# Down matrices of 29 experts requested from ScalarE's queue instead of SyncE's

## The reference

```
x = x + merged @ w_out
h2 = rmsnorm(x)
# 32 experts, the best 4 for each token, softmax weights over the 4
gu  = h2[tokens of e] @ w_gu[e] + b_gu[e]           # 1024 -> 2048
hid = (clip(lin) + 1) * g * sigmoid(1.702 * g)      # g, lin: halves of gu, clamped at 7
y   = hid @ w_down[e] + b_down[e]                   # 1024 -> 1024
x   = x + sum over the 4 experts of weight * y
out = rmsnorm(x)
```

## Time and profile before

| | |
|---|---|
| median of 3 executions | 1201.55 us (1201.41 to 1204.66) |
| the profiled execution | 1201.84 us, its span 1200.0 us |
| TensorE busy | 1113.0 us, 93% |
| VectorE, ScalarE busy | 401.2 and 246.9 us |
| SyncE's queue | 449.79 of the 452.07 MB moved |
| transfers of expert matrices | 83 up (52 of 4096 KB, 17 of 2048, 14 of 1024) and 72 down (56 of 2048 KB, 16 of 1024) |
| mean granted clock of TensorE | 0.98 of full speed |

### The profile page before, as it was taken

One profiled execution on the slowest core, in us unless ns is written; L12 is line 12 of the kernel. 1 busy time (PEld: TensorE's weight loads), 2 busy tenths in 40 slices (PEclk: granted clock), 3 DMA queues, 4 the chain that ended last, 5 costly groups with the idle time before them and its releaser, 6 DMA issues.

```text
span 1200.0 us, 14789 instructions
## 1 busy us (share of the span) xinstructions
PE 1113.0 (93%) x6062; PEld 590.1 (49%) x6062; DVE 401.2 (33%) x695; ACT 246.9 (21%) x389; POOL 4.5 (0%) x10
## 2 busy tenths in 40 slices
PE   8999999999999989898989989889899998998995
PEld 8999999985444333333333333333344333333331
DVE  6767554563322222222222222222222222222212
ACT  6344674433111111111111111111111111111112
POOL 0000000000000000000000000000000000000000
PEclk9999999999999999999999999999999999999998
DMA  9984343689999999999999999999999999999994
GB/s 332 349 280 142 116 160 132 251 313 372 415 421 430 431 430 430 431 431 430 431 432 429 430 436 433 426 435 431 427 435 429 429 434 423 432 435 424 427 404 193
DMA packets 60119, 452.07 MB, mean 377 GB/s; under 512 B 3458, under 2 KB 34423, under 8 KB 40247
## 3 DMA queue, kind: packets, MB, share of 16 engines
q1 hardware_dynamic: 59408, 449.79, 91.0%
q0 software_dynamic: 560, 1.74, 0.5%
q10 hardware_dynamic: 119, 0.08, 0.0%
HBM read 450.53 MB, written 1.06 MB: 376 GB/s over the span
## 4 chain that ended last, share of the span: by engine, by line
PE 48%; DMA 48%; SPq 1%; issue 1%; DVE 1%; ACT 1%; DVEq 0%; ACTq 0%
DMA dring<-in_w_down_dram 41%; PE bank L1111 17%; PE bank L1433 13%; PE bank L1394 11%; DMA ring<-in_w_gu_dram 6%; PE bank L1361 2%; DMA ring<-in_w_mem_kv_dram 1%; PE bank L1312 1%; PE bank L1336 0%; PE bank L1340 0%; PE bank L1201 0%; PE bank L1181 0%; PE bank L1409 0%; PE bank L1212 0%; ACT w_high L469 0%
## 5 line engine op out<-in xcount | busy, mean ns | idle before, releaser
L1394 PE MATMUL bank<-ring,region_x 128*64 128x512 f32 x2048 | 456.3, 597 | 8.0 <-DMA ring<-in_w_gu_dram 8.0
L1433 PE MATMUL bank<-dring,region_r 128*64 128x512 f32 x1024 | 245.6, 631 | 60.2 <-DMA dring<-in_w_down_dram 59.9
L1394 PEld LDWEIGHTS bank<-ring,region_x 128*64 128x64 f32 x2048 | 141.2, 137 | 282.6 <-issue 266.1
L1433 PEld LDWEIGHTS bank<-dring,region_r 128*64 128x64 f32 x1024 | 74.2, 144 | 229.6 <-issue 135.3
L1111 PE MATMUL bank<-hT_high,w_high 128*128 128x256 f32 x384 | 110.1, 287 | 1.4 <-DVE hT_low L708 1.4
L1111 PE MATMUL bank<-hT_low,w_high 128*128 128x256 f32 x384 | 108.6, 283 | 0.0
L1111 PE MATMUL bank<-hT_high,w_low 128*128 128x256 f32 x384 | 108.6, 283 | 0.0
L1050 DVE SCALAR_TENSOR_TENSOR y_parts<-bank,region_r,y_parts 64x512 fp32r<-64x512 f32 x32 | 23.8, 744 | 249.5 <-ACT y_parts L642 249.5
L716 DVE TENSOR_TENSOR w_low<-ring,w_high 128x2048 fp32r<-128x2048 f32 x39 | 89.3, 2289 | 53.3 <-ACT w_high L469 53.1
L1031 DVE TENSOR_SCALAR region_r<-bank 128x512 f32<-128x512 f32 x32 | 22.1, 692 | 252.3 <-PE bank L1394 252.3
L469 ACT ACTIVATE w_high<-ring 128x2048 fp32r<-128x2048 f32 x39 | 74.5, 1912 | 62.5 <-PE bank L1111 57.8
(11 more groups left out here) (237 smaller groups left out, 887.9 us busy)
## 6 DMA issues: line engine op xcount, KB each, us to landing
ring<-in_w_gu_dram SPq DMA_DIRECT2D x52, 4096.0 KB, 26.3
dring<-in_w_down_dram SPq DMA_DIRECT2D x56, 2048.0 KB, 24.7
ring<-in_w_gu_dram SPq DMA_DIRECT2D x17, 2048.0 KB, 11.5
ring<-in_w_in_dram SPq DMA_DIRECT2D x26, 1024.0 KB, 11.9
dring<-in_w_down_dram SPq DMA_DIRECT2D x16, 1024.0 KB, 12.3
ring<-in_w_gu_dram SPq DMA_DIRECT2D x14, 1024.0 KB, 8.2
ring<-in_w_out_dram SPq DMA_DIRECT2D x4, 1024.0 KB, 5.0
ring<-in_w_mem_kv_dram SPq DMA_DIRECT2D x3, 1024.0 KB, 11.9
```

Of the source, the lines that this page charges most:

```text
L1394: last = mm(ps[64 * half:64 * half + 64, :], xg[u // 2][:, c, 64 * (u % 2):64 * (u % 2) + 64], ring[:, slot0 + c, k * F + half * 512:k * F ...
L1433: last = mm(y_ps[64 * half:64 * half + 64, :], lhsT, dring[:, c // 2, at:at + 512], start=(c == 0), stop=(c == KC - 1))
```

## The change

SyncE no longer asks for the down matrices of experts 1 to 29; it asks for the up matrices alone, and for the downs of experts 0, 30 and 31 as before. The interleaved order of experts 22 to 29 is gone with them. ScalarE asks for the down matrix of expert s+1 in `weighted_high(s)`, when it has waited for the whole down product s, between its two weighting instructions, as two transfers of two slots each. Its loop ends two rounds earlier, and the last rounds are written out without requests. In TensorE's stream only the counts change that `down` waits for, as down matrix 1 no longer comes in single slots.

```diff
@@ -388,31 +388,14 @@
             for c, n in ((0, 1), (1, 1), (2, 1), (3, 1), (4, 1), (5, 1), (6, 2)):
                 sp.wait_ge(pieces_used, N_MIX + (expert - 2) * KC + c + n)
                 up_chunks(expert, slot0 + c, c, n)
-        expert_down(1, 1, 1)
-
         with sp.Fori(0, more * (E // 2) + (E // 2 - 7)) as i:
             expert_up((i * 2 + 4) % E, 8, i * 16 + (N_MIX - RING + 33))
-            expert_down((i * 2 + 2) % E, i * 8 + 5)
             expert_up((i * 2 + 5) % E, 0, i * 16 + (N_MIX - RING + 41))
-            expert_down((i * 2 + 3) % E, i * 8 + 9)
 
         ups, downs = more * (KC * E) + (N_MIX - RING + 1), more * (DRING * E) + (1 - DRING)
-
-        def half_up(expert, h):
-            sp.wait_ge(pieces_used, ups + expert * KC + 4 * h + 3)
-            up_chunks(expert, 8 * (1 - expert % 2) + 4 * h, 4 * h, 4)
-
-        for expert in range(E - 10, E - 5):
-            half_up(expert, 0)
-            expert_down(expert - 2, downs + (expert - 2) * DRING)
-            half_up(expert, 1)
-        expert_down(E - 7, downs + (E - 7) * DRING)
-        for expert in range(E - 5, E - 2):
-            half_up(expert, 0)
-            half_up(expert, 1)
-            expert_down(expert - 1, downs + (expert - 1) * DRING)
+        for expert in range(E - 10, E - 2):
+            expert_up(expert, 8 * (1 - expert % 2), ups + expert * KC)
         expert_up(E - 2, 8, ups + (E - 2) * KC, 2)
-        expert_down(E - 3, downs + (E - 3) * DRING)
         for c, n in ((0, 2), (2, 2), (4, 2), (6, 1), (7, 1)):
             sp.wait_ge(pieces_used, ups + (E - 1) * KC + c + n - 1)
             up_chunks(E - 1, c, c, n)
@@ -634,21 +617,30 @@
             act.wait_ge(y_ready, s + 1)
             act.activation(unused, y_ps[:, 0:TT * P], ACT.Copy, accum_out=w_slot).then_inc(w_slot_ready, 1)
 
-        def weighted_high(s):
+        def weighted_high(s, following):
 
             act.wait_ge(downs_used, (s + 1) * DRING)
             act.wait_ge(w_slot_ready, s + 1)
             act.activation(y_parts[0:64, 0:512], y_ps[0:64, :], ACT.Copy, scale=w_slot[0:64, :])
+            if following is not None:
+                for m in range(2):
+                    act.dma_start(dring[:, 2 * m:2 * m + 2, :].rearrange("p k n -> p (k n)"),
+                                  a["w_down"][0, bass.ds(following, 1), m * 512:(m + 1) * 512, :]
+                                  .rearrange("e (p k) n -> p (e k n)", k=4)).then_inc(down_in[2 * m], 16)
             act.activation(y_parts[64:128, 512:1024], y_ps[64:128, :], ACT.Copy, scale=w_slot[64:128, :])\
                 .then_inc(y_high, 1)
 
         sigmoid_of(0)
-        with act.Fori(0, more * E + (E - 1)) as s:
+        with act.Fori(0, more * E + (E - 3)) as s:
             hidden_and_slots(s)
             sigmoid_of(s + 1)
-            weighted_high(s)
+            weighted_high(s, (s + 1) % E)
+        for s in range(E - 3, E - 1):
+            hidden_and_slots(more * E + s)
+            sigmoid_of(more * E + (s + 1))
+            weighted_high(more * E + s, None)
         hidden_and_slots(more * E + (E - 1))
-        weighted_high(more * E + (E - 1))
+        weighted_high(more * E + (E - 1), None)
 
 
         act.activation(norm[:, 3, 4:6], norm[:, 1, 2:4], ACT.Sqrt)
@@ -1468,7 +1460,7 @@
                 s = i * 4 + u
                 nxt = (i, u + 1) if u < 3 else (i + 1, 0)
                 up(*nxt, False, lambda: small_products(i, u))
-                down(s, int(u > 0))
+                down(s, 0)
                 begin(s + 2)
                 next_half(*nxt)
 
@@ -1482,13 +1474,13 @@
                     for half in range(2):
                         mm(acc[t][half][:, :], wexpT[:, t * P:(t + 1) * P], b_down[:, half * 512:half * 512 + 512],
                            start=False, stop=False)
-            down(s, 1 + u // 2)
+            down(s, u // 2)
             if u < 2:
                 begin(s + 2)
             if u < 1:
                 next_half(i, u + 1)
         small_products(i, 3, 1)
-        down(i * 4 + 3, 3)
+        down(i * 4 + 3, 2)
 
         pe.wait_ge(y_ready, more * E + (E + 1))
         pe.wait_ge(scaT_sb, more * E + (E + 1))
```

## The result

The changed kernel takes 1236.1 us (median of 4, 1233.7 to 1239.2) against 1202.7 for the kernel before: a ratio of 1.0281, 95% interval 1.0257 to 1.0305, slower by 33 us. Forecast was slower, by 19, with a range up to 1225; the loss is 1.8 times the forecast.

The account below looks back on a forecast made before the run. The 16 DMA engines were taken to bound the expert stage; 19 us later at down product 30, 1.5 of them from the start, gave a span of 1200 + 19, or 1220.5 us on the median's scale, range 1205 to 1225.

Parts of the forecast that it names:

- What bounds the kernel, and R: DMA engines bound the expert stage; R is up-matrix data outstanding, in us of DMA time, when a down product ends.
- R(28): Up-matrix data outstanding at the end of down product 28: 35.4 us before, forecast 12.9 (10 to 14).
- the sum for the start: At the start, down matrix 1 is asked for later: DMA idle for 0 to 2.6 us, 1.5 taken.
- Lead in the tail: Tail: down product 30 starts at 1185.8 instead of 1166.75, 19 us later, 1.5 of them from the start.
- the prediction's first rival: Requests are served in order of asking, two queues or one: down product 30 at 1186.9, time 1221.7; chance 0.12.
- Turns by packet: Queues alternate by packet: down matrices get one third of the rate beside up halves; 1216 to 1224, chance 0.55.
- Turns by whole transfers: Queues alternate up half, down half: loss 11.9 us, time 1213.5; chance 0.10.
- equal bytes: Queues share by bytes: downs always in time, TensorE waits for up second halves; +4.8, time 1206.4; chance 0.10.
- a higher rate: Two queues hide gaps between packets: 436 against 431 GB/s, 9.4 us; 1197 with the lead kept, chance 0.08.
- Issue on ScalarE: Two requests per expert between the weighting halves: y_parts 0.7 to 1.4 us later, 5.1 us of cover, cost 0.
- The steady state: Main loop: outstanding up data fall from 15.6 to about 6 us, swing between some 2 and 8; DMA stays busy.
- the prediction's rule: Main loop: down gets a third until outstanding ups are gone, all the rate until 11.7 us, then a third again.

Follow-up runs that it names:

- e11: The changed kernel run once more unaltered, for a second profile: 1233.3 us.
- e1: The kernel before, one queue, with SyncE keeping the plain order of its loop from expert 22 on: 1219.0 us, ratio 1.0134.
- e4: The changed kernel, but SyncE asks for the down matrices from expert 20 on in the interleaved order of the kernel before: 1217.1 us, ratio 1.0113.
- e2: The changed kernel with up matrices from expert 4 on in pieces of 2 slots, 16 KB packets like the downs: 1210.6 us, ratio 1.0067.
- e3: The changed kernel with ScalarE's down matrices in single slots, 8 KB packets beside 32 KB up packets: 1269.6 us, ratio 1.0579.
- e5: The changed kernel, but ScalarE asks for the first half of the next down matrix in the middle of the down product: 1220.7 us, ratio 1.0162.
- e7: The kernel before, one queue, with up matrices from expert 4 on in pieces of 2 slots: 1205.8 us, ratio 1.0038.
- e8: The kernel before, one queue, with both down halves asked for only after the whole down product: 1201.5 us, ratio 1.0001.
- e9: The kernel before with b_down asked for early on ScalarE's queue and the 8 bias products moved ahead of down product 29: 1201.1 us, ratio 0.9988.

## Why the prediction was right in kind and too small

**What bounds the kernel, and R.** Right. Down product 30 started 1201.9 - 1156.8 = 45.1 us after the end of down product 28, forecast 45.7, without a wait. R(28) = 1177.2 - 9.7 - 1156.8 = 10.7, forecast 12.9 (10 to 14); that is by landing, as in the prediction. One small slip in the sum for the start: 1024 KB that land in 5.3 us take 2.9 us more than their bytes, not 2.6.

**Lead in the tail.** Right: forecast 17.5 us, measured 19.2 and, in e11, 20.6. e1 and e4 show that it is the order of requests: without it one queue loses 18.2 us, and with it, and with the downs from expert 20 on back in SyncE's queue, the changed kernel loses none. No run has that order on two queues. As the prediction's first rival had it, serving in order of asking would have cost about the same in the tail, so the right size here doesn't tell the two apart; the alternating rows, e2 and e3 exclude it as a description of the two queues.

**Turns by packet.** Right, and the step that I called the weakest. 81 rows against 82, and the time follows the packets' sizes in e2 and e3. Turns by whole transfers and equal bytes are excluded by the same rows; a higher rate didn't come (424 GB/s against 431). The Trainium skill (DMA: Bandwidth & Descriptors, section Queues, rings and completion order) says that an engine goes round its queues packet by packet, and the trace agrees: 81 against 82 from 776 to 786 us, one row of a transfer at each turn. How many of the page's descriptors such a row is, 9 to 17 or fewer, no run here can show.

**Issue on ScalarE.** Right: two requests take 0.84 us, up to 2.4 in some steps, and TensorE never waits for y_parts inside the loop.

**The steady state: R "between some 2 and 8, never to zero: the DMA stays busy".** This is the step that failed. The term for a DMA without work was 1.5 us, the start alone; measured are 16.0 us of late bytes (10.8 in e11), 14.5 us more, of the 16 by which the profiled execution missed the forecast. R at the request ran up to 10.0 and down to 0.0, in e11 up to 9.9 and down to 0.5.

Two things in the working of the steady state were off. First, the prediction gave the ups their two thirds as soon as they are asked for again. In the trace their first row came 3.5 to 3.7 us later, so at R of 6.7 and 7.6 the down matrix was there after 21.8 and 23.9 us, where the prediction's rule gives 27.5 and 29.2 from the request. The short waits let R grow past 8. Second, at R = 9.7 the down matrix had a third to its end, 31.0 us, the wait was 10.1, and the half product behind it took 6.42 us instead of 3.65. That step took 38.2 us from request to request, and 9.7 + 29.2 - 38.2 leaves R = 0.7. (The rule's own worst case, a third all the way, is 29.2 us from the request and 8.4 us late; the "2.3 us late" of the prediction is for R = 6 alone.) Two of the signs named ahead failed with it: the rate didn't stay near 431 from 360 us on, and ScalarE's transfers took 7.7 to 33.6 us and not 11 to 28.

That R near zero is what loses the bytes fits e5 and e2: e5, where R stays at 5.1 or more, has 4.0 us of late bytes, and e2, where R grows to 28, has 3.5, about what smaller packets cost in one queue (e7, 4.0). The size varies by itself: the same kernel lost 16.0 us in one execution and 10.8 in another. That the tail came out right says nothing for the steady state, since any R from 2 to 8 gave 10 to 14 there. Why single engines fall behind (three ahead of 385.4, one ahead of 686.4) stays open; the two waits with such engines cost 6.0 and 4.2 us of bytes, the three without 1.8 to 2.8.

## What to carry to other kernels

When transfers are the bound, a kernel still has a second quantity to lose: the lead, how little of the landed data is unused when the last bytes come. It is set by the order of the requests, and a change can leave the rate alone and cost 18 us at the end. Two queues share the engines by turns of packets (81 rows against 82), so before a stream is given a queue of its own, compare its bytes per partition row with those beside it: the larger rows win, and a transfer with a due time belongs at its place in one queue, unless it is small.

## What was not expected of the hardware

- Behind a backlog, 3.5 us of later asking cost nothing in one queue (e8, ratio 1.0001) and some 15 us in a second one (changed kernel against e5).
- A transfer on the slower side of the turns doesn't always end on all engines at once: 13 were through by 376.7 us, the last three at 382.1, 382.3 and 384.9.
- A queue that was empty while the other was busy got its first row 3.5 to 3.7 us after the request; with the other queue empty or nearly so it was 0.9 to 1.0 us.
- A transfer of 128 KB on a queue of its own passed a backlog of more than 20 us in 7.2 us (e9).
